# Three weight rings moved from the start of a kernel's SBUF to its end, on one Trainium2 core

## What is computed

```python
xn = rmsnorm(x, norm1_g)
x = x + hybrid_mixer(xn, ...)          # w_in, conv, attention, mix_w_out
hn = rmsnorm(x, norm2_g)
# peer, per token, 8 heads, top 16 of 128*128 experts
q = hn @ w_q
s = einsum('thpd,hpnd->thpn', q, sub_keys)
...
h = einsum('thkd,td->thk', u_tab[e], hn)
act = gelu(h) * gate
y = einsum('thk,thkd->td', act, v_tab[e])
```

## Time and profile before

| | |
|---|---|
| median of 3 runs | 1006.47 us (1006.11 to 1007.08) |
| span of the profiled execution, first to last instruction | 1004.5 us |
| TensorE busy | 1000.0 us, 7310 matmuls |
| VectorE, ScalarE, GpSimd busy | 787.3, 526.7, 459.9 us |
| loads of weight tiles | 332, of 512 KB each |
| read from HBM | 180.33 MB, 183 GB/s over the span |

### The profile page before, as it was taken

The page is one execution under the profiler, slowest core; times in us unless marked ns, Lnnn a source line. Parts: engine busy times, 40 slices in busy tenths (PEclk is TensorE's granted clock), DMA queues, the critical chain, the costliest instruction groups (busy, mean ns, idle before and its releaser), DMA issues.

```text
span 1004.5 us, 21094 instructions
## 1 busy us (share of the span) xinstructions
PE 1000.0 (100%) x7310; PEld 905.6 (90%) x7310; DVE 787.3 (78%) x1368; ACT 526.7 (52%) x853; POOL 459.9 (46%) x198
## 2 busy tenths in 40 slices
PE   9999999999999999999999999999999999999998
PEld 9998999999999999998888888888888888888887
DVE  6999784868899992088888888998888876767764
ACT  6654877644544444545555555644444444455443
POOL 4654455656689999863333444200000004443442
PEclk9999999999999999999999999999999999999999
DMA  7694445554455565555555555565555556565562
GB/s 242 216 303 148 142 147 187 193 189 147 166 185 177 182 194 195 177 167 167 169 180 173 167 173 179 180 201 169 178 175 172 183 171 191 188 201 189 188 199 93
DMA packets 52618, 181.93 MB, mean 181 GB/s; under 512 B 5943, under 2 KB 9155, under 8 KB 52452
## 3 DMA queue, kind: packets, MB, share of 16 engines
q1 hardware_dynamic: 52292, 181.16, 55.3%
q10 hardware_dynamic: 288, 0.27, 0.1%
HBM read 180.33 MB, written 3.43 MB: 183 GB/s over the span
## 4 chain that ended last, share of the span: by engine, by line
PE 100%; ACT 0%; issue 0%; POOL 0%; POOLq 0%
PE bank L1242 37%; PE bank L1564 34%; PE bank L1499 12%; PE bank L1501 6%; PE bank L1513 3%; PE bank L1343 2%; PE bank L1257 1%; PE bank L1475 1%; PE bank L1266 1%; PE bank L1590 1%; PE bank L1359 1%; PE bank L1382 0%; PE bank L1370 0%; PE bank L1273 0%; PE bank L1320 0%; PE bank L1310 0%
## 5 line engine op out<-in xcount | busy, mean ns | idle before, releaser
L354 POOL TENSOR_TENSOR lo<-raw,hi 128x1024 fp32r<-128x1024 f32 x184 | 457.0, 2496 | 530.5 <-ACT hi L335 530.1
L335 ACT CAST hi<-raw 128x1024 fp32r<-128x1024 f32 x332 | 347.7, 1048 | 219.1 <-PE bank L1564 183.6
L1242 PE MATMUL bank<-norm_space,hi 128*128 128x256 f32 x1600 | 282.5, 280 | 0.1
L1564 PE MATMUL bank<-hi,norm_space 128*128 128x512 f32 x1008 | 273.9, 391 | 0.0
L1242 PEld LDWEIGHTS bank<-norm_space,hi 128*128 128x128 f32 x1600 | 243.7, 188 | 1.8 <-issue 1.1
L1242 PE MATMUL bank<-norm_space,lo 128*128 128x256 f32 x800 | 223.2, 279 | 0.0
L1564 PEld LDWEIGHTS bank<-hi,norm_space 128*128 128x128 f32 x1008 | 187.9, 188 | 38.2
L354 DVE TENSOR_TENSOR lo<-raw,hi 128x1024 fp32r<-128x1024 f32 x148 | 188.7, 1275 | 39.7 <-ACT hi L335 39.7
L1499 PE MATMUL bank<-norm_space,hi 128*128 128x512 f32 x512 | 179.7, 393 | 0.0
L1564 PE MATMUL bank<-lo,norm_space 128*128 128x512 f32 x504 | 155.3, 389 | 0.0
L1242 PEld LDWEIGHTS bank<-norm_space,lo 128*128 128x128 f32 x800 | 150.4, 188 | 0.0
(11 more groups left out here) (190 smaller groups left out, 949.6 us busy)
## 6 DMA issues: line engine op xcount, KB each, us to landing
raw<-u_tiles SPq DMA_DIRECT2D x128, 512.0 KB, 3.3
raw<-v_tiles SPq DMA_DIRECT2D x128, 512.0 KB, 3.3
raw<-front SPq DMA_DIRECT2D x76, 512.0 KB, 3.9
toeplitz<-bias_row SPq DMA_DIRECT2D x6, 384.0 KB, 7.6
bias<-toeplitz SPq DMA_DIRECT2D x12, 128.0 KB, 3.5
resid<-x_t SPq DMA_DIRECT2D x2, 512.0 KB, 4.7
qk<-sub_keys SPq DMA_DIRECT2D x1, 1024.0 KB, 8.4
y<-act SPq DMA_DIRECT2D x3, 256.0 KB, 2.0
```

Of the source, the lines that this page charges most:

```text
L335: act_e.copy(hi[:, s, :], raw[:, s, :]).then_inc(hi_ready, 1)
L354: eng.tensor_tensor(lo[:, s, :], raw[:, s, :], hi[:, s, :].bitcast(F32), ALU.subtract)\
L1242: ins = pe.matmul(dst, w_[:, s, u * P:(u + 1) * P], x_[:, k, :], start=first and i == 0 and p_ == 0, stop=last and i == n - 1 and p_ == 2)
L1564: ins = pe.matmul(bank[2 * c + half][:, :], a_[:, j, c * P:(c + 1) * P], v_[:, j, half * 512:(half + 1) * 512], start=False, stop=False, s ...
```

## The change

The three calls that allocate the rings stand after all others. No instruction is touched.

```diff
@@ -175,9 +175,6 @@
         bank = [ctx.enter_context(nc.psum_tensor(f"bank{i}", [P, 512], F32)) for i in range(8)]
 
 
-        raw = sb("raw", [P, RING, D])
-        hi = sb("hi", [P, RING, D], F32R)
-        lo = sb("lo", [P, RING, D], F32R)
         norm_space = sb("norm_space", [P, KB * 2 * T + SHIFT], F32R)
@@ -229,6 +226,9 @@
         eqB = sb("eqB", [P, TOK // PAIR, HALF, PAIR], F16)
         half_sum = sb("half_sum", [P, 2, T])
         ohB = sb("ohB", [P, 2, TOK // PAIR, 2, HALF, PAIR], F16)
+        raw = sb("raw", [P, RING, D])
+        hi = sb("hi", [P, RING, D], F32R)
+        lo = sb("lo", [P, RING, D], F32R)
```

## The result

The changed kernel takes 1012.39 us (median of 3 runs, 1012.05 to 1012.97) against 1006.47: a ratio of 1.0058, 95% interval 1.0038 to 1.0077. It is slower by 0.6%, clear of the noise, and the time is the one forecast. The way there is not: the profile shows a gain and a loss larger than the sum.

A forecast was written before the change was run, and what follows sets the result against it. The prediction took TensorE's matmul-to-matmul interval as the bound. Products and wide keys +4.2 us and value pass +1.5 us gave +5.7 us on 1006.5, so 1012 us, range 1001 to 1018.

The forecast's parts named there:

- What bounds the kernel: Whole span: only TensorE's interval from one matmul to the next, summed over 7310 matmuls, sets the end.
- Step 3: Casts, low parts and loads at the rings' new address: cost nothing, covered by TensorE's 2.80 us a tile.
- rival 3: First half of the keys: GpSimd's low parts slow down and become the bound, +6.4 us, 1013 us; chance 0.04.
- rival 1: All ring accesses: placement is nothing, 1006.5 us within 1.5 us; chance 0.33.
- Step 4: Front value tiles, 144 operations of L1343 whose moving side alone changes: under 0.2 us.
- Step 1: 3144 products of L1242 and 1024 wide key matmuls, loaded operand now off by 32 bytes: 1.0 ns each, +4.2 us.
- rival 2: TensorE's matmuls: faster, new ring-to-token distance removes a stall between its two reads, -5 to -11 us, 995 to 1001; chance 0.25.
- Step 2: Value pass, 1536 matmuls whose moving operand is now off by 32 bytes: 1.0 ns each, +1.5 us.
- if one shortens while the other grows: Stretches of 1440 products and 792 value-pass matmuls: opposite changes would mean operand distance, not either's own start, sets the effect.

## Why the prediction was right, and by which steps it was not

The number is right: 1012 forecast, 1012.39 measured. Two of the steps that make it are wrong, and they cancel.

**What bounds the kernel** held: the interval from matmul to matmul, and nothing beside it. **Step 3** (casts, low parts and loads cost nothing) held too, but for one wait of 0.2 us; GpSimd stayed at 2.4 us, so rival 3 is out, and rival 1 (nothing) with it. **Step 4** (the six tiles of L1343, under 0.2 us more) was as small as put: by the chain they became some 0.2 us shorter.

**Step 1**, "+4.2 us" from 1.0 ns on 4168 matmuls with bounds of nothing and 1.6 ns, has the wrong sign for 3144 of them. In the long stretch the products gained 3.3 ns (116.7 to 113.4), and the stages that hold them became 6.84 us shorter. That is rival 2 for the products, and 3.3 ns is more than its price of a quarter to a half of 5.1 ns. The 512 wide pairs lost 6 ns each and their stage 3.02 us, more than the 2 x 1.0 ns a pair of the step.

**Step 2**, "the same 1.0 ns", with an upper bound of 4.5, measured 6.6 ns: the value pass became 9.91 us longer, where +1.5 was put.

-6.84 + 3.02 + 9.91 is +6.1 us, and +4.2 + 1.5 was +5.7. The agreement is luck. The error behind both steps was to read each operand's own start off the rows, because the operands that start off by 32 bytes happened to be in the dearer pairs. In the rows of before, only the distances 32 and 0 (and 224, with the roles swapped, in L1343) occur, so no row could bound the others: the nearest row is no bound where the quantity doesn't rise or fall steadily. The text did name the sign by which this would show: "if one shortens while the other grows, the effect goes by the distance of the two operands and not by either's own start". So it was.

The Trainium skill ("TensorE: Matmul & The Clock Gate", Step-by-step: what each phase is for) says that the moving operand and the weight load have independent read ports and don't take bandwidth from each other. The table speaks against the second half of that: with the same instructions, the distance between the two operands is worth up to 7.6 ns of 227 and up to 6.7 of 113. That both reads meet in some part of SBUF is the plainest reading, but it is argued: what the runs show is the dependence on the distance, and that the place of the rings, a common shift and the place of raw don't enter.

**Open.** Why the levels lie as they do over the distances, and why a run can hold two levels at one distance. In the changed kernel the 1440 products on `nrm` run at 113.4 ns and the 312 on `xg`, at the same distance of 192, at 36.75 / 312 = 117.8 ns. Before the change the 312 ran at 116.7:

```profile
217.43 36.41 PE bank L1242 x312
```

So not even all products gained. The earlier trace rows have 116.7 and 117.8 for one form, and the stretch of 96 there, 11.31 us, takes 11.21 with 160 bytes of padding, at the same distance:

```profile
430.60 11.21 PE bank L1243 x96
```

So something beside the distance takes part in which level a stretch has. It may be how the stretch starts, but no run here isolates it.

## What to carry to other kernels

Where TensorE is never idle, the starting bytes of the loaded and of the moving operand within 256 are a tuning parameter, per pair: print the distances, measure each pair's interval in its longest stretch and in a short one beside it, and set each pair by itself, with padding that costs no instruction. A move of one tensor shifts every pair that it is in; here one pair gained and two lost, and moving the third tensor after it (the activations, by 96 bytes) took back the loss of the value pass and kept the gain of the products, while the wide pairs still pay theirs (353 ns, some 3 us). A total that agrees with a forecast proves none of its terms: read each stage's own length.

## What was not expected of the hardware

- TensorE's interval depends on (moving start - loaded start) within 256 bytes. In float32r, with loads of 128x128 and in the long stretches, it is 113.4 to 120.1 ns for 256 columns, 347 to 353 for a pair of 512 and 256, 226.8 to 234.4 for 512.
- There is no order that holds for all shapes. Distance 0 gives 226.8 ns in the value pass and 120.0 in the products; 192 gives 113.4 in the products, 353 in the wide pairs and 233.4 in the value pass.
- The distance doesn't fix the level of the products alone: at 192 and at 64 some stretches run at 113.4 ns and others at 117.8.
- Some 160 KB of distance, a common shift of 96 bytes and a shift of the DMA's target are worth nothing: ratios 1.000, 1.000 and 1.0003, and stretches equal to 0.01 us.
